# Branch and out stages of a hybrid attention/mLSTM layer: 576 token columns split in halves of 288, against 512 prompt columns apart from 64 decode columns, with the out projection computed by tokens

## What is computed

```python
mod = silu(c) @ w_ada + b_ada                    # shift, scale, gate: per sequence
h = rmsnorm(x, norm_pre) * (1 + scale) + shift
u = h @ w_in                                     # q, k, v, z of attention; q, k, v, o, z of the mLSTM;
                                                 # its two gates; g_a and g_m (2048 columns each)
y_a = (rmsnorm(att) * (1 - lam_init) * silu(z_a)) @ w_br_a    # 1024 x 2048
y_m = (sigmoid(o_m) * rmsnorm(hm) * silu(z_m)) @ w_br_m       # 1024 x 2048
y = (sigmoid(g_a) * y_a + sigmoid(g_m) * y_m) @ w_out         # 2048 x 2048
out = x + gate * rmsnorm(y, norm_post)
```

## Time and profile before

| | us |
|---|---|
| median of 3 runs | 2185.51 (2181.76 to 2190.83) |
| the profiled execution | 2187.54 |
| its span, from the first to the last instruction | 2185.9 |
| PE busy in the span | 2045.4 (94%), 15108 matmul records |
| DVE, ACT, POOL busy | 800.1, 621.5, 161.1 |
| mean granted clock of TensorE | 0.968 |

### The profile page before, as it was taken

How to read it: one execution, slowest core, us unless ns; L and a number is a source line. 1 busy time by engine, 2 the same in 40 slices (tenths; PEclk the granted TensorE clock), 3 DMA queues, 4 the chain that set the end, 5 groups by cost and what they waited for, 6 DMA issues and landing times.

```text
span 2185.9 us, 37865 instructions
## 1 busy us (share of the span) xinstructions
PE 2045.4 (94%) x15108; PEld 1895.0 (87%) x15108; DVE 800.1 (37%) x1554; ACT 621.5 (28%) x1108; POOL 161.1 (7%) x281
## 2 busy tenths in 40 slices
PE   5999999988898888999999999999999999989996
PEld 3779999877787877778889999999999999989996
DVE  3455334466632224443333432222233223243334
ACT  3212222334344433322322322222222222222221
POOL 2000001000020000001321000000000000110000
PEclk8999999999999999999989999999999999999998
DMA  9772332221143331122333333343343343472222
GB/s 342 254 252 74 103 99 77 59 87 44 44 150 121 121 100 43 47 57 76 107 89 88 82 81 108 116 112 106 116 111 113 110 117 111 128 218 83 73 77 101
DMA packets 177618, 240.30 MB, mean 110 GB/s; under 512 B 14497, under 2 KB 145697, under 8 KB 175785
## 3 DMA queue, kind: packets, MB, share of 16 engines
q1 hardware_dynamic: 157472, 177.24, 28.2%
q0 software_dynamic: 17808, 61.53, 8.3%
q10 hardware_dynamic: 2242, 0.19, 0.1%
HBM read 220.02 MB, written 18.89 MB: 109 GB/s over the span
## 4 chain that ended last, share of the span: by engine, by line
PE 72%; issue 12%; DVE 9%; ACT 5%; DMA 2%; POOL 0%; DVEq 0%; ACTq 0%; POOLq 0%
PE gemm L489 60%; PE bank_a L489 4%; PE bank_s L489 3%; PE bank_o L489 3%; DVE e_map L1640 1%; DVE w_lo L1358 1%; ACT L1022 1%; ACT w_hi L1022 1%; DVE mx L1641 1%; DMA y_back<-y_scratch 1%; ACT e_map L1022 1%; PE bank_s L724 1%; DMA ada_in<-in_w_ada 1%; DVE em_b L1737 1%; PE bank_s L514 0%
## 5 line engine op out<-in xcount | busy, mean ns | idle before, releaser
L489 PE MATMUL gemm<-h_hi,w_hi 128*128 128x288 f32 x3584 | 806.8, 307 | 37.5 <-DVE z_act L1747 17.7
L489 PE MATMUL gemm<-h_hi,w_lo 128*128 128x288 f32 x3584 | 778.9, 299 | 0.0
L489 PE MATMUL gemm<-h_lo,w_hi 128*128 128x288 f32 x3584 | 778.2, 299 | 0.0
L1358 DVE TENSOR_TENSOR w_lo<-w_raw,w_hi 128x512 fp32r<-128x512 f32 x512 | 353.6, 692 | 1096.3 <-ACT w_hi L1022 1095.7
L489 PEld LDWEIGHTS gemm<-h_hi,w_hi 128*128 128x128 f32 x3584 | 587.8, 193 | 101.4 <-issue 80.2
L1022 ACT ACTIVATE w_hi<-w_raw 128x512 fp32r<-128x512 f32 x512 | 321.3, 629 | 1059.8 <-PE gemm L489 1045.1
L489 PEld LDWEIGHTS gemm<-h_lo,w_hi 128*128 128x128 f32 x3584 | 588.4, 192 | 0.0
L489 PEld LDWEIGHTS gemm<-h_hi,w_lo 128*128 128x128 f32 x3584 | 588.0, 192 | 0.0
L489 PE MATMUL gemm<-brm,w_hi 128*128 128x288 f32 x512 | 90.7, 300 | 6.6 <-DVE y_mix L1843 6.6
L489 PEld LDWEIGHTS gemm<-brm,w_hi 128*128 128x128 f32 x512 | 77.0, 193 | 6.8 <-DVE y_mix L1843 6.8
L1022 ACT ACTIVATE e_map<-e_map,nmx 128x128 f32<-128x128 f32 (+3 forms) x64 | 35.4, 554 | 118.8 <-DVE nmx L1642 118.8
(11 more groups left out here) (401 smaller groups left out, 1482.3 us busy)
## 6 DMA issues: line engine op xcount, KB each, us to landing
w_raw<-in_w_in SPq DMA_DIRECT2D x384, 256.0 KB, 2.8
ada_in<-in_w_ada SPq DMA_DIRECT2D x32, 1024.0 KB, 9.9
ada_g<-in_w_ada POOLq DMA_DIRECT2D x32, 512.0 KB, 4.8
w_raw<-in_w_out SPq DMA_DIRECT2D x64, 256.0 KB, 2.9
k_page<-in_cache_k POOLq DMA_DIRECT2D x16, 512.0 KB, 5.5
v_page<-in_cache_v POOLq DMA_DIRECT2D x16, 512.0 KB, 4.6
w_raw<-in_w_br_a SPq DMA_DIRECT2D x32, 256.0 KB, 2.8
w_raw<-in_w_br_m SPq DMA_DIRECT2D x32, 256.0 KB, 2.8
```

The costliest lines, as they stand in the source:

```text
L489: return nc.tensor.matmul(out, lhsT, rhs, start=start, stop=stop, skip_group_check=True)
L1358: V.tensor_tensor(w_lo[:, slot], w_raw[:, slot], w_hi[:, slot], ALU.subtract).then_inc(lo_ready, 1)
```

## The change

**Granules.** From the branch stage on a slot holds 128 rows x 512 columns (2 KB in one piece per row), the same 256 KB. `wide_granule` does, for each of 4 column blocks, the 3 products with 512 prompt tokens moving, 12 matmuls. The 64 decode tokens are done the other way round (`s_part`): high and low part side by side are one stationary operand of 128 columns, and the 512 weight columns move, once with `w_hi` (128 stationary columns) and once with `w_lo` (the high part alone, 64 columns), into `bank_s`. That is 14 matmuls of 512 columns per granule. For this `bra`, `brm` and `y_all` hold a block as prompt high, decode high, decode low, prompt low; for `h_hi` and `h_lo` the decode parts are copied together once (`h_smp`, in pass 30).

**Branch stage.** 4 iterations of 48 granules instead of 8 of 24. The four banks of `gemm` hold four column blocks of the prompt. The decode result has tokens on the partitions and its high and low share on different ones; ACT copies it to SBUF (`copy_s`), and in the next pass four f32 matmuls with `fold` (two identity matrices, one above the other) add the shares and transpose (`fold_features`). `g_a` and `g_m` have four blocks; the mix is made in `g_a`. Of the y blocks 12 go by DRAM and come back one per granule; the last four are split straight from `g_a` in the first pass of the out stage.

**Out stage by tokens.** 4 passes of 16 granules: the tokens are stationary (`h[:, rows]`), `w_out` moves, and the result has tokens on the partitions. No transposes follow. ACT squares a bank with a sum over its columns (`y_ssq`), DVE multiplies it by the gate into `y_tok`. The gate is needed as rows for that: `gates_of` makes them on PE once per pass from `mod_g` and `g_exp`. `fold_tokens` adds up the decode shares.

**Before them.** `smp_new` takes one half r of the value dimension for both lots of sequences (32 rows of the array each) instead of both halves of one lot (64 rows), and the old states are stored after both. `c_pad_g` goes; `c_t` with 9 columns is used directly. Passes 28 to 31 and the branch and out stages are written out for ACT and DVE, and the branch and out stages for PE, where loops stood.

```diff
+            def wide(slot):
+                return (w[:, slot].rearrange("p t c -> p (t c)") for w in (w_hi, w_lo))
+            def s_part(slot, both, first, last):
+                wh, wl = wide(slot)
+                mm(bank_s[:, 0, :], both, wh, start=first, stop=False)
+                mm(bank_s[0:NS, 0, :], both[:, 0:NS], wl, start=False, stop=last).then_inc(gemm_used, 1)
+            def wide_granule(m, slot, of, first, last):
+                hi, lo, both = of
+                for b in range(4):
+                    if first:
+                        pe.wait_ge(bank_free[b // 2], V0 + 32 + (2 * m - 1 + b % 2 if m else 0))
+                    wh, wl = (w[:, b * P:(b + 1) * P] for w in wide(slot))
+                    for n, (w, h) in enumerate(((wh, hi), (wh, lo), (wl, hi))):
+                        done = mm(gemm[:, b // 2, b % 2, :], w, h, start=first and n == 0, stop=last and n == 2)
+                    if last:
+                        done.then_inc(block0_done, 1)
+                if first and m:
+                    pe.wait_ge(s_copied, m)
+                s_part(slot, both, first, last)
+            def fold_features(m):
+                pe.wait_ge(s_copied, m + 1)
+                if m:
+                    pe.wait_ge(s_used, m)
+                for b in range(4):
+                    done = mm(bank_s[:, 1, b * NS:(b + 1) * NS], s_copy[:, b * P:(b + 1) * P], fold[:])
+                done.then_inc(s_folded, 1)
...
-            def branch_pair(i):
-                for j in range(FSPLIT):
...
+            def branch_quad(i):
+                for j in range(FGRAN):
+                    m, _, kind, kt, n = mat_of(S_F + FGRAN * i + j)
+                    pe.wait_ge(lo_ready, S_F + FGRAN * i + j + 1)
+                    of = h_parts(kt) if kind in ("ga", "gm") else parts(bra if kind == "ya" else brm, kt)
+                    wide_granule(m, j % RING, of, kt == 0, kt == n - 1)
+                    if kt == 1 and m:
+                        fold_features(m - 1)
+                    if j % 6 == 3:
+                        ada_g_round(2 * i + j // 24, j // 6 % 4)
+                    if j in (23, 47):
+                        ada_rows(mod_row_g, ADA_CHUNKS + 2 * i + j // 24, 2)
...
+            def gates_of(q):
+                pe.wait_ge(gate_rows, 3 * q + 1)
+                for b in range(4):
+                    mm(bank_o[:, b * P:(b + 1) * P], mod_g[:, 4 * q + b, 0:1].to_broadcast([P, P]), ident[:])
+                for b in range(4):
+                    done = mm(bank_a[0:NS, b * P:(b + 1) * P], g_exp[:, b, :], ident[:])
+                done.then_inc(gate_rows, 1)
+            def fold_tokens(q):
+                m = 4 * FQ + q
+                pe.wait_ge(s_copied, m + 1)
+                pe.wait_ge(s_used, m)
+                mm(bank_s[0:NS, 1, :], fold[:], s_copy[:]).then_inc(s_folded, 1)
...
+                    for tt in range(NT):
+                        if first:
+                            pe.wait_ge(bank_free[tt // 2], V0 + 32 + 2 * m - 1 + tt % 2)
+                        rows = slice(tt * P, (tt + 1) * P)
+                        for n, (h, w) in enumerate(((hi, wh), (lo, wh), (hi, wl))):
+                            done = mm(gemm[:, tt // 2, tt % 2, :], h[:, rows], w, start=first and n == 0, stop=last and n == 2)
...
-            def smp_new(hd, lot):
-                pe.wait_ge(kw_ready, 2 * hd + lot + 1)
-                for r in range(2):
-                    done = mm(bank_s[:, r, :], v_mls[0:NS, NT, hd * DV + r * P:hd * DV + (r + 1) * P],
-                              kw_s[:].rearrange("p b k -> p (b k)"))
+            def smp_new(hd, r):
+                pe.wait_ge(kw_ready, hd + 1)
+                for lot in range(2):
+                    rows = slice(lot * NS // 2, (lot + 1) * NS // 2)
+                    done = mm(bank_s[:, lot, :], v_mls[rows, NT, hd * DV + r * P:hd * DV + (r + 1) * P],
+                              kw_s[rows].rearrange("p b k -> p (b k)"))
...
+            def mix(kind, m):
+                for b in range(4):
+                    dve.wait_ge(block0_done, V0 + 32 + 4 * m + b + 1)
+                    dve.wait_ge(bank_free[b // 2], V0 + 32 + 2 * (m - 2) + b % 2 + 1)
+                    g = (g_a if kind == "ya" else g_m)[:, b, 0:TP]
+                    ins = V.scalar_tensor_tensor(g, g, 1.0, gemm[:, b // 2, b % 2, :], ALU.add, ALU.mult)
+                    ins.then_inc(bank_free[b // 2], 1)
+                    if kind == "ym":
+                        dve.wait_ge(bank_free[b // 2], V0 + 32 + 2 * m + b % 2 + 1)
+                        V.tensor_tensor(g_a[:, b, 0:TP], g_a[:, b, 0:TP], g, ALU.add).then_inc(mix_ready, 1)
+            def gated(q, tt):
+                dve.wait_ge(yq_done, 5 * q + tt + 1)
+                dve.wait_ge(gate_rows, 3 * q + 3)
+                V.tensor_tensor(y_tok[:, tt, q * QW:(q + 1) * QW], gemm[:, tt // 2, tt % 2, :], y_gate[:, 0, :], ALU.mult).then_inc(bank_free[tt // 2], 1)
```

More of the change, by code:

```diff
@@ L992, in _ @@
             pe.wait_ge(pad_ready, 2)
-            with pe.Fori(0, 8) as i:
-                branch_pair(i)
-            def out_pair(p, first):
-                for g in range(NG):
-                    pe.wait_ge(lo_ready, S_G + NG * p + g + 1)
-                    if first:
-                        pe.wait_ge(y_lo_made, 2 * g + 2)
-                    granule(g % RING, h_hi, h_lo, 2 * g, g == 0, g == NG - 1, V0 + 64 + p)
-                    if g < 2 and not first:
-                        to_tokens(y_gp[:, g, :], (bank_free[g], V0 + 64 + p), (yt_sb, 2 * p - 1) if g else (yq_done, 2 * p), yt_ps)
@@ L1006, in _ @@
[L1006 to L1016 removed]
+            pe.wait_ge(smp_made, 1)
@@ new lines, in _ @@
+            for i in range(FQ):
+                branch_quad(i)
+            def gates_of(q):
[10 more added lines that the diff above has]
+                mm(bank_s[0:NS, 1, :], fold[:], s_copy[:]).then_inc(s_folded, 1)
@@ new lines, in out_quad @@
+            def out_quad(q):
+                m = 4 * FQ + q
+                for kt in range(KT):
+                    slot, first, last = kt % RING, kt == 0, kt == KT - 1
+                    pe.wait_ge(lo_ready, S_G + KT * q + kt + 1)
+                    if not q:
+                        pe.wait_ge(y_lo_made, kt + 1)
+                    wh, wl = wide(slot)
+                    hi, lo, both = parts(y_all, kt)
+                    for tt in range(NT):
[4 more added lines that the diff above has]
+                            done = mm(gemm[:, tt // 2, tt % 2, :], h[:, rows], w, start=first and n == 0, stop=last and n == 2)
+                        if last:
+                            done.then_inc(block0_done, 1)
+                    if first:
+                        pe.wait_ge(s_copied, m)
+                    s_part(slot, both, first, last)
+                    if kt == 1:
+                        fold_tokens(q - 1) if q else fold_features(m - 1)
+                    if kt == 9:
+                        gates_of(q)
@@ L1019, in _ @@
+            for q in range(FQ):
+                out_quad(q)
+            fold_tokens(FQ - 1)
         @nc_block.scalar
@@ L1863, in out_pair @@
-            def out_pair(p, first, last):
-                for g in range(NG):
-                    n = g + LOOKAHEAD
-                    if not (last and n >= NG):
-                        split_lo(n % RING, S_G + NG * p + n)
-                    if first and g == 2:
-                        y_lo(14)
-                        y_lo(15)
+                src = y_back[:, blk % 2, :] if blk < 12 else g_a[:, blk - 12, :]
+                V.scalar_tensor_tensor(y_all[:, blk, T + NS:2 * T], src[:, 0:TP], 0.5, y_all[:, blk, 0:TP], ALU.mult, ALU.subtract)
```

483 lines of the change are left out of this document (252 added, 231 removed).

## The result

The changed kernel takes 2165.87 us (median of 4 runs, 2164.54 to 2167.11), the kernel before 2183.64 beside it (4 runs, 2180.39 to 2190.83): a ratio of 0.9915, 95% interval 0.9895 to 0.9935. In a later series of five rounds it was 2166.02 and 0.9944 (0.9928 to 0.9960). 18 us less, where 46 were forecast.

What follows compares the result with a forecast made beforehand. PE's matmul stream, busy 94% of the span, was taken as the bound. Granules -46, added +33, gone -26 and smp_new -7 gave -46 from 2187.5, 2139.5 on the median, said as 2140 us, range 2120 to 2190.

Steps and rivals of the forecast that it cites:

- granules -46: Branch and out stages: 512-column float32r matmul at 216 ns, granule 3.02 us instead of 3.20, over 256 granules -46 us.
- rival 1: The 13 ns come once per float32r matmul: 227 ns, granule 3.17, -7 us on granules; total 2179; chance 0.25.
- Rival 2: The 13 ns come per column: 237 ns, granule 3.32, +30 us on granules; total 2216, slower; chance 0.09.
- Rival 3: Each 64-stationary-column decode matmul changes the array's division, 0.33 us per granule, +84; total 2224, slower; chance 0.05.
- Rival 4: Turnovers of the four banks cost 1.3 us more at each of 20 ends; PE waits 25 us or more; 2166; chance 0.09.
- folds 0.9 each: PE, fold_features 16 times: eight small f32 records of 0.11 us, 0.9 us each, +14 us.
- The adaLN rounds, 0: PE, branch stage: 32 rounds as before, 0 us change; c_t with 9 columns still takes a quarter of the array each.
- The waits at the end of ym: Each bank takes a mix and an add on DVE, so PE waits 1.6 to 1.8 us, four times: +7 us.
- Gone, -26: PE: y_gp transposes -8, bank waits at out-pass ends -9, y_mix wait and squeezed y blocks behind it -9 us.
- the wait for y_mix: 6.6 us, and some 4 behind it from two y blocks per granule on ACT and DVE; -9, 1 or 2 left.
- The condition set ahead, 820 to 850 us: Branch and out stages together must come out between 820 and 850 us, or all of the prediction is wrong.
- State stage, -7: smp_new's two 32-row matmuls overlap on different array rows, 8 x 0.85 = -7 us; the 0.89 clock can move it.

Runs made afterwards that it cites:

- m_width: Changed kernel, single accumulations with other widths, stationary operands, rows, banks or types of prompt matmul; 512-column float32r 227 ns between starts, bf16 216; no total time given.
- s_pairs: Kernel before, order kept, smp_new's two matmuls reading 32 rows each on different rows of the array: 2172.56 us, ratio 0.9924.
- s_order: Kernel before with the changed state stage's new order, smp_new still two 64-row matmuls one after the other: 2175.23 us, ratio 0.9928.
- m_width2: Changed kernel, second set of prompt matmul widths and types, plus an inserted 64-column matmul; float32r 205, 147, 112 ns at 448, 320, 192 columns; no total time given.
- n_fold: Changed kernel with TensorE's folds replaced by ACT copies and DVE adds, only the finished y turned on TensorE: 2150.26 us, ratio 0.9870 to before.

## Why the prediction was wrong, step by step

- **The step that failed is "granules -46".** It took 3 ns over the columns from the plain f32 rows for a float32r matmul. Measured: 227 ns, a granule of 3.193 instead of 3.200, 256 x 0.007 = -1.8 us, less than even rival 1's -7. The 13 ns (11 to 18 by width) come once per float32r matmul, at 256 to 512 columns alike: rival 1, at 0.25. Ten matmuls fewer per granule give 133 ns, and 256 more columns (14 x 512 against 24 x 288) take 107. 14 x 226.7 would be 3.174; the other 19 ns lie around the decode matmul with 64 stationary columns, where neighbours start 228 to 236 ns apart.
- The argument "against" rival 1 was the fault: the f32 rows are records of 0.43 us for 512 columns, where float32r takes 0.227, and they could not speak for another type. The rows that could, 288 columns of float32r, showed 13.4 over.
- Rival 2 (per column) falls with the table: 13 ns over the columns at 256 and 14 at 512. Rival 3 (0.33 us at each 64-column float32r matmul) falls: the granule holds no step of 0.3, and with 64 stationary columns throughout the distance was 229 ns (m_width). For plain f32 records with 64 stationary columns such a step was measured, 0.33 us a call of gates_of; that it comes of how the array is divided, no run shows. Rival 4 falls: the evictions cost 3.0 us in all, where it wanted 25 and more.
- **Added on PE:** folds 0.9 each, measured 0.84 to 0.90: +13.9, right. The adaLN rounds, 0: eight records in 0.62 us with 9 stationary columns (1547.96), in 0.64 with 32; what share of the array they take, no run shows. gates_of 5.33 - 3.19 = 2.1 four times: +8.6, right. fold_tokens 4.41 - 3.19 = 1.2 three times: +3.7, right. The waits at the end of ym: +7 forecast, 3.0 measured (1.4 of it idle). DVE was costed too dear there: the first mix begins at 1429.61, right behind that step's split and 1.5 us before the granule's end, not after it.
- **Gone, -26:** before had 57.8 us over its granules in the two stages (256 x 3.200 in 877.0). After has 60.2 over 256 x 3.193, and 29.2 of them are the added parts (13.9 + 8.6 + 3.7 + 3.0), so 26.8 have gone. Right as a sum, with one cause wrong in it. Behind the wait for y_mix the text saw some 4 us of y blocks squeezed in. What stands there is one granule of 5.50 us, 2.3 too long, at a granted clock of 0.55:

```profile
1923.00:1928.50 5.50, 5.50 (x25) 5.50 (x26) 2.69 (x4) 1.36 (x2) 1.15 (x3) 0.55 0.60 183
```

- Both stages: -1.8 + 29.2 - 26.8 = +0.6 us, where -39 was forecast. The condition set ahead, 820 to 850 us, failed by 28.
- **State stage, -7:** measured -22.0. The overlapping pair did give 0.85 a call. The other 15 us are the granted clock, 0.89 to 0.98, of which the text said only that it can move the term by some us. It is most of what makes the kernel faster at all. The two errors, +44 and -15, partly hide each other in the total: that there is a gain of 18 us at all is luck as far as this forecast goes, since most of its cause is not in it.
- Tail 22.0 for 22.7, the brm wait 3.9 for 4.4, y blocks without a wait, the state refetch without a wait: right.

What stays open: which of the small matmuls of the state stage bring the lower clock (s_pairs has pairs of 32 rows and showed 0.93, s_order has 64 rows and showed 0.95, and no run changed the 8-column records), which of the moved steps raises it, and why it falls in some executions of one and the same code and not in others.

## What to carry to other kernels

Take the overhead per matmul from rows of the same type (here 13 ns in float32r against 2 or 3 in the other two), and price a new tiling as matmuls x overhead + columns before anything else; here both were moved against each other and nothing was left. Where a stage's clock is below 1.00, multiply its length with it: that separated work from clock here (154, 154 and 153 us for the same pairs at 0.93, 0.98 and 0.90), and most of an edit's effect may be in the second, as here. When one engine is the bound at 94 to 99%, its smallest side jobs (here 20 folds of 0.9 us) are worth more than its main loop's shape, as long as the others sit idle beside it.

## What the runs showed of the hardware that was not expected

- At a granted clock of 1.00 a float32r matmul of N columns took 0.417 N + 13 ns at 256 to 512 columns (11 to 18 by width), a bf16 one 0.417 N + 2 to 3, a plain f32 record 0.833 N + 2 (m_width, m_width2). At 0.50 float32r had nothing over 0.833 N: 512 columns in 427 ns (m_width, 32 rows), 288 in 240.
- Below 256 moving columns a float32r matmul with a 128x128 stationary operand did not get much shorter: 112 ns at 192 columns, some 0.12 us for an inserted one of 64 (m_width2). At a clock of 0.50, 128 and 64 columns both took 213 ns (m_width), as long as 256 columns at 0.833 ns each.
- The granted clock was 0.50 for long stretches with PE busy throughout. The windows of m_width with 128 and with 64 moving columns, with 64 rows, and with 32 rows (both with 512 columns), PE busy throughout:

```profile
1406.00:1441.00 35.00, 35.00 (x147) 30.35 (x146) 8.22 (x15) 5.67 (x9) 2.93 (x5) 0.50 0.41 119
1476.00:1511.00 35.00, 35.00 (x153) 29.70 (x151) 8.87 (x16) 6.29 (x10) 1.45 (x2) 0.50 0.29 83
...
1690.00:1720.00 30.00, 30.00 (x130) 20.21 (x128) 6.68 (x11) 6.65 (x12) 0.75 (x1) 1.00 0.26 89
1725.00:1770.00 45.00, 45.00 (x108) 29.27 (x108) 8.11 (x14) 4.40 (x7) 0.75 (x1) 0.50 0.18 55
```

  With 128 and 64 moving columns and with 32 of 128 rows it was 0.50, with 64 rows and 512 columns 1.00.
- ACT read PSUM partitions 64 to 127 and wrote SBUF partitions 0 to 63, and the other way round, at next to no extra price: in n_fold such copies of 64x256 took 0.38 us each, those that stayed on their partitions 0.36 to 0.38.
